# A decoder step on one core: a longer and earlier warm-up of TensorE, the sample rows' transposes placed between the two prompt tiles, and a final norm with its order and owners changed

## What is computed

```python
def rmsnorm(x, g):
    y = x * lax.rsqrt(jnp.mean(x * x, axis=-1, keepdims=True) + EPS)
    return y * g

hp = jnp.concatenate([meta, x_prompt], axis=1)     # 16 + 256 rows
hs = x_sample                                      # 8 rows
mp, Sp, Pp = mixer(rmsnorm(hp, norm_mix), ...)     # w_in, retention, pooling, w_out
hp = hp + mp
hp = hp + moe(rmsnorm(hp, norm_ffn), ...)          # 32 experts, top 4, clamped SwiGLU
...                                                # the same for hs, with the running state
y_prompt = rmsnorm(hp[:, N_META:], norm_final)
y_sample = rmsnorm(hs, norm_final)
```

## Time and profile before

| | |
|---|---|
| median of 3 runs | 1202.28 us (1201.06 to 1202.86) |
| the profiled execution | 1203.43 us, its span in the profile 1201.6 us |
| TensorE (PE) busy | 1154.7 us, 96% of the span |
| VectorE, ScalarE, GpSimd busy | 307.2, 160.0, 62.8 us |
| DMA | 455.09 MB, mean 379 GB/s |
| the chain that ended last | PE 68%, DMA 30%, SP's queue 1% |

### The profile page before, as it was taken

One profiled execution on the slowest core, in us unless ns is written; L12 is line 12 of the kernel. 1 busy time (PEld: TensorE's weight loads), 2 busy tenths in 40 slices (PEclk: granted clock), 3 DMA queues, 4 the chain that ended last, 5 costly groups with the idle time before them and its releaser, 6 DMA issues.

```text
span 1201.6 us, 13661 instructions
## 1 busy us (share of the span) xinstructions
PE 1154.7 (96%) x5403; PEld 572.8 (48%) x5403; DVE 307.2 (26%) x699; ACT 160.0 (13%) x314; POOL 62.8 (5%) x92
## 2 busy tenths in 40 slices
PE   8999999999999999999989998989999989999997
PEld 7888788886434334333434333434333434333332
DVE  4363511232122122221221221213121212121222
ACT  2122111002010111111110101010101100110112
POOL 3252600000000000000000000000000000000000
PEclk9999999999999999999999999999999999999999
DMA  9762788476999999999999999999999999999996
GB/s 321 231 228 90 261 327 319 142 315 264 424 418 427 424 434 428 425 434 425 425 434 426 431 428 434 421 435 426 436 425 433 421 433 429 433 428 429 428 419 241
DMA packets 63728, 455.09 MB, mean 379 GB/s; under 512 B 4321, under 2 KB 35501, under 8 KB 42688
## 3 DMA queue, kind: packets, MB, share of 16 engines
q1 hardware_dynamic: 59168, 439.60, 88.3%
q0 software_dynamic: 4176, 14.34, 3.5%
q10 hardware_dynamic: 344, 0.61, 0.1%
HBM read 448.65 MB, written 6.11 MB: 378 GB/s over the span
## 4 chain that ended last, share of the span: by engine, by line
PE 68%; DMA 30%; SPq 1%; issue 0%; ACT 0%; DVE 0%; DVEq 0%; ACTq 0%
PE psum L1087 24%; DMA ring<-in_w_down 21%; PE psum L1016 19%; PE psum L1098 10%; DMA ring<-in_w_gate_up 8%; PE psum L1174 5%; PE psum L1208 2%; PE psum L1154 1%; SPq L591 1%; PE psum L1164 1%; PE psum L1209 1%; PE psum L1183 1%; DMA ring<-in_x_prompt 0%; PE psum L897 0%; PE psum L1088 0%
## 5 line engine op out<-in xcount | busy, mean ns | idle before, releaser
L1087 PE MATMUL psum<-ring,x_T 128*64 128x512 f32 x1004 | 455.7, 600 | 9.6 <-DMA ring<-in_w_gate_up 8.8
L1088 PE MATMUL psum<-ring,x_T 128*64 128x512 f32 x994 | 450.6, 600 | 0.0
L1087 PEld LDWEIGHTS psum<-ring,x_T 128*64 128x64 f32 x1004 | 131.0, 137 | 275.1 <-issue 252.4
L1098 PE MATMUL psum<-ring,act_T 128*64 128x512 f32 x960 | 216.0, 602 | 25.1 <-DMA ring<-in_w_down 25.1
L1016 PE MATMUL psum<-ring 128*128 128x264 f32 (+1 forms) x768 | 181.7, 392 | 0.6 <-DMA ring<-in_w_in 0.6
L1016 PEld LDWEIGHTS psum<-ring 128*128 128x128 f32 x768 | 143.2, 190 | 30.2 <-ACT qk L1445 2.1
L1098 PEld LDWEIGHTS psum<-ring,act_T 128*64 128x64 f32 x960 | 70.2, 138 | 159.4 <-issue 139.6
L1088 PEld LDWEIGHTS psum<-ring,x_T 128*64 128x64 f32 x994 | 129.6, 137 | 0.0
L1906 DVE TENSOR_TENSOR h_raw<-psum,params 128x512 f32<-128x512 f32 x32 | 22.1, 691 | 295.0 <-PE psum L1154 295.0
L1923 DVE TENSOR_TENSOR z_T<-z_T,psum 128x264 f32<-128x264 f32 x112 | 43.0, 425 | 205.5 <-PE psum L1209 205.5
L1174 PE MATMUL psum<-normed,one_hot 128*128 128x512 f32 x168 | 74.4, 592 | 0.0
(11 more groups left out here) (268 smaller groups left out, 751.3 us busy)
## 6 DMA issues: line engine op xcount, KB each, us to landing
ring<-in_w_gate_up SPq DMA_DIRECT2D x32, 4096.0 KB, 31.7
ring<-in_w_gate_up SPq DMA_DIRECT2D x59, 2048.0 KB, 29.8
ring<-in_w_down SPq DMA_DIRECT2D x56, 2048.0 KB, 33.3
ring<-in_w_in SPq DMA_DIRECT2D x21, 1024.0 KB, 6.6
ring<-in_w_down SPq DMA_DIRECT2D x12, 1024.0 KB, 26.8
spare<-in_w_gate_up SPq DMA_DIRECT2D x5, 1280.0 KB, 36.8
out<-ring POOLq DMA_DIRECT2D x9, 512.0 KB, 9.5
ring<-in_state_ret POOLq DMA_DIRECT2D x8, 512.0 KB, 7.2
```

The source lines that it names most:

```text
L1087: mm(psum[0:CAP, 2 * j + n], x, gate, start=first, stop=final)
L1088: last = mm(psum[CAP:P, 2 * j + n], x, up, start=first, stop=final)
L1098: last = mm(psum[j * CAP:(j + 1) * CAP, 4 + n], hidden[:, j, 4 * h + i], w, start=h == 0 and i == 0, stop=h == 1 and i == 3)
```

## The change

Three places change. `WARM` goes from 6 to 10, and GpSimd clears `k_few` first of all, then `small` and the third tile. The loads of the sample and meta rows move from SP's queue, behind the prompt tiles, to ACT's queue, behind `norm_mix` and ahead of the other three small vectors; SP goes from the prompt tiles to `w_in` at once. Their transposes on TensorE (L954) and the scaling on VectorE (L1693) move between the tiles: after tile 0 and ahead of tile 1. In the final norm the sample piece of the second half comes before that of tile 1; the first square roots and the first reciprocal are those of tiles 0 and 2, and tile 0 is scaled right behind them. Tile 1 is split: ACT scales its first half, VectorE makes its second half in one operation out of PSUM. The sample rows' first half is weighted by VectorE early and scaled by GpSimd, and only their second half is made by VectorE at the end.

```diff
-WARM = 6
+WARM = 10
...
-        Y_HALVES = [(n, t) for n in range(2) for t in (0, 1, 2)]
+        Y_HALVES = [(n, t) for n in range(2) for t in ((0, 1, 2), (0, 2, 1))[n]]
...
-            sp.wait_ge(cleared, 2)
-            sp.dma_start(tok[0:NS, 2, :], x_sample.rearrange("b s d -> (b s) d")).then_inc(x_in[2], 16)
-            sp.dma_start(tok[NS:NS + NM, 2, :], meta).then_inc(x_in[2], 16)
...
+            nc.gpsimd.memset(k_few[:, :], 0.0).then_inc(few_cleared, 1)
             nc.gpsimd.memset(small[:, 0:4], 1.0).then_inc(cleared, 1)
+            nc.gpsimd.memset(tok[:, 2, :], 0.0).then_inc(cleared, 1)
             nc.gpsimd.memset(y_sums, 0.0).then_inc(zeroed, 1)
-            nc.gpsimd.memset(tok[:, 2, :], 0.0).then_inc(cleared, 1)
             nc.gpsimd.memset(place[:, :, :], FAR).then_inc(zeroed, 1)
-            nc.gpsimd.memset(k_few[:, :], 0.0).then_inc(few_cleared, 1)
...
+            pool.wait_ge(y_weighted, 3)
+            pool.wait_ge(y_rstd, 1)
+            nc.gpsimd.tensor_scalar(normed[0:NS, 2, 0:512], normed[0:NS, 2, 0:512], rstd[0:NS, 2:3], None,
+                                    ALU.mult).then_inc(y_s_ready, 1)
...
+            act_e.dma_start(rows[0:8, 0:P], ins["norm_mix"].rearrange("l (a p) -> (l a) p", p=P)).then_inc(norm_in, 16)
+            act_e.wait_ge(cleared, 2)
+            act_e.dma_start(tok[0:NS, 2, :], x_sample.rearrange("b s d -> (b s) d")).then_inc(x_in[2], 16)
+            act_e.dma_start(tok[NS:NS + NM, 2, :], meta).then_inc(x_in[2], 16)
+            for o, name, n in ((8, "ret_gn", 8), (16, "pool_scale", 4), (20, "norm_ffn", 8)):
...
-                    for s in (0, 1) if i == 4 else (2,):
+                    for s in (0, 2) if i == 4 else (1,):
                         A(rms[:, s:s + 1], y_sums[:, 3 + s:4 + s], ACT.Sqrt, bias=y_base[:, s:s + 1],
                           scale=1.0 / D).then_inc(y_rms, 1)
-                act_e.wait_ge(y_weighted, 4)
-                act_e.wait_ge(y_rstd, 1)
-                A(normed[:, 1], normed[:, 1], ACT.Copy, scale=rstd[:, 1:2]).then_inc(y_ready, 1)
-                act_e.wait_ge(y_ready, 1)
+                act_e.wait_ge(y_weighted, 2)
+                act_e.wait_ge(y_rstd, 2)
+                A(normed[:, 1, 0:512], normed[:, 1, 0:512], ACT.Copy, scale=rstd[:, 1:2]).then_inc(y_ready, 1)
+                act_e.wait_ge(y_ready, 2)
...
-                    if t == 2:
-                        continue
-                    V.tensor_tensor(normed[:, t, c], y_tok(t)[:, c], w_final[:, c], ALU.mult).then_inc(y_weighted, 1)
-                    if i == 3:
+                    if i < 4:
+                        rows_n = TILES[t][1]
+                        V.tensor_tensor(normed[0:rows_n, t, c], y_tok(t)[0:rows_n, c], w_final[0:rows_n, c], ALU.mult).then_inc(
+                            y_weighted, 1)
+                    elif i == 4:
                         dve.wait_ge(y_rms, 2)
-                        V.reciprocal(rstd[:, 0:2], rms[:, 0:2]).then_inc(y_rstd, 1)
-                    if i == 4:
-                        dve.wait_ge(y_weighted, 3)
+                        V.reciprocal(rstd[:, 0:3:2], rms[:, 0:3:2]).then_inc(y_rstd, 1)
+                        dve.wait_ge(y_weighted, 4)
                         dve.wait_ge(y_rstd, 1)
                         V.tensor_scalar(normed[:, 0], normed[:, 0], rstd[:, 0:1], None, ALU.mult).then_inc(
                             y_first_ready, 1)
                 dve.wait_ge(y_rms, 3)
-                V.reciprocal(rstd[:, 2:3], rms[:, 2:3]).then_inc(y_rstd, 1)
+                V.reciprocal(rstd[:, 1:2], rms[:, 1:2]).then_inc(y_rstd, 1)
                 dve.wait_ge(y_rstd, 2)
-                for n in range(2):
...
+                V.scalar_tensor_tensor(normed[:, 1, c], y_tok(1)[:, c], rstd[:, 1:2], w_final[:, c], ALU.mult,
+                                       ALU.mult).then_inc(y_ready, 1)
+                V.scalar_tensor_tensor(normed[0:NS, 2, c], y_tok(2)[0:NS, c], rstd[0:NS, 2:3], w_final[0:NS, c], ALU.mult,
+                                       ALU.mult).then_inc(y_s_ready, 1)
```

More of the change, by code:

```diff
@@ L951, in _ @@
                     pe.transpose(psum[:, 2, 0:KD], rows[0:KD, 0:P], ident[0:KD, 0:KD]).then_inc(norm_turned, 1)
-            pe.wait_ge(x_in[2], 32)
-            for k in range(KD):
-                last = pe.transpose(psum[:, 3, k * few:(k + 1) * few], tok[0:few, 2, k * P:(k + 1) * P],
-                                    ident[0:few, 0:few])
-            last.then_inc(few_turned, 1)
+                    pe.wait_ge(x_in[2], 32)
+                    for k in range(KD):
+                        last = pe.transpose(psum[:, 3, k * few:(k + 1) * few], tok[0:few, 2, k * P:(k + 1) * P],
+                                            ident[0:few, 0:few])
+                    last.then_inc(few_turned, 1)
             def turn_roots():
@@ L1403, in _ @@
             act_e.dma_start(consts[:, 0:EARLY], ins["consts"][:, 0:EARLY]).then_inc(ident_in, 16)
-            for o, name, n in ((0, "norm_mix", 8), (8, "ret_gn", 8), (16, "pool_scale", 4), (20, "norm_ffn", 8)):
-                act_e.dma_start(rows[o:o + n, 0:P], ins[name].rearrange("l (a p) -> (l a) p", p=P)).then_inc(
-                    rows_in if o else norm_in, 16)
-            act_e.wait_ge(cleared, 1)
+            act_e.dma_start(rows[0:8, 0:P], ins["norm_mix"].rearrange("l (a p) -> (l a) p", p=P)).then_inc(norm_in, 16)
[3 more added lines that the diff above has]
+            for o, name, n in ((8, "ret_gn", 8), (16, "pool_scale", 4), (20, "norm_ffn", 8)):
+                act_e.dma_start(rows[o:o + n, 0:P], ins[name].rearrange("l (a p) -> (l a) p", p=P)).then_inc(rows_in, 16)
             step(A(small[:, 1:2], small[:, 0:1], ACT.Sqrt))
@@ L1690, in _ @@
                     V.tensor_copy(norm_mix, psum[:, 2, 0:KD]).then_inc(norm_ready, 1)
[L1691 to L1695 removed]
+                    dve.wait_ge(norm_ready, 1)
+                    dve.wait_ge(few_turned, 1)
+                    V.tensor_tensor(x_raw[:, :, NPR:NA], psum[:, 3, 0:KD * few].rearrange("p (k c) -> p k c", k=KD),
+                                    norm_mix.rearrange("p (k c) -> p k c", c=1).broadcast_to([P, KD, few]),
+                                    ALU.mult).then_inc(few_scaled, 1)
             for n in range(2):
```

9 lines of the change are left out of this document (1 added, 8 removed).

## The result

| | before | changed |
|---|---|---|
| median (19 runs of each) | 1202.19 us (1201.06 to 1202.96) | 1203.94 us (1202.08 to 1206.78) |
| ratio, 95% interval | | 1.0017 (1.0011 to 1.0023) |
| the profiled execution, its span | 1203.43, 1201.6 us | 1203.30, 1201.4 us |

By the interval of the ratio the changed kernel is 1.3 to 2.8 us **slower**; by the medians it is 1.75 us. That is within the 0.2% (2.4 us) of the prediction's middle class, but it has the other sign than the forecast of 1201.5, and 1203.94 lies outside the range that ended at 1203.6.

What follows compares the result with a forecast made beforehand. TensorE was taken to bound the kernel to 275 us and the weights' stream from 300 us. Start -0.40 and end -0.35 gave 1202.28 - 0.75 = 1201.5 us (chance 0.55), range 1200.2 to 1203.6.

Steps and rivals of the forecast that it cites:

- the prediction's middle class: Whole kernel: time within 0.2% (2.4 us) of before, neither faster nor slower by more; chance 0.91.
- What bounds the kernel: TensorE to 275 us, weights' stream from 300 us; a microsecond's shift of the start should come out at the end.
- The start: First 9 us: first real matmul at 8.70 instead of 9.10, -0.40 us; ends -0.50 and +0.51.
- X: Start: time when second prompt tile and few rows have both landed; taken as 6.95 us, ends 6.79 and 7.86.
- Rival 2: Start: few rows land late on ACT's queue; with X = 8.0 first matmul at 9.75, +0.65, total 1202.6; chance 0.12.
- The clock: Start: TensorE's clock rises from 1.2 to 2.4 GHz, taken to rise a microsecond sooner with the earlier warm-up.
- The warm-up: Start: begins 1.0 us sooner, at about 1.0, with twenty instructions; tile 0 starts at about 5.2.
- The end: Last 8 us, final norm: stores 0.45, 0.08 and 0.34 us sooner, taken as -0.35; ends -0.45 and -0.08.
- my lower end of 0.08: End: smallest gain expected, -0.08 us, where only the second store counts.
- Rival 1: End: GpSimd gets the port lock before VectorE; end +1.2, with the start's -0.4 +0.8, total 1203.1; chance 0.12.
- my price for 8x512 alone: End: GpSimd's scaling of the sample rows' first half, 1.55 us when running alone.
- The sums: Whole kernel: added-up gains and losses of the cases, from -0.95 to +1.9 us, the latter with rivals 1 and 2 together.

Runs made afterwards that it cites:

- e7: Changed kernel with the few rows (sample and meta) back on SP's queue, ahead of `w_in`: 1202.15 us, ratio 0.9994 to the kernel before.
- e12: Changed kernel plus six idle matmuls, into an unused PSUM bank, ahead of the wait for the few rows: 1204.02 us, ratio 1.0017 to before.
- e2: Kernel before with only the change's final norm, old start: 1201.88 us, ratio 1.0000.
- e1: Changed kernel with the old final norm, so the change's start alone: 1204.04 us, ratio 1.0016 to the kernel before.
- e3: Kernel before with only the few rows' loads moved from SP's to ACT's queue: 1204.38 us, ratio 1.0016.
- e15: Changed kernel unaltered, profiled once more: one execution, 1203.80 us.
- e9: Changed kernel, but SP waits for GpSimd's clearing of `q_only`, so `w_in` is issued behind the few rows: 1202.39 us, ratio 0.9999 to before.
- e8: e7 plus four idle matmuls ahead of the wait for the few rows (output not the reference's): 1202.28 us, ratio 1.0005 to the kernel before.
- e6: Changed kernel plus six idle matmuls over part of tile 0's transposed rows, ahead of the few rows' wait (output wrong): 1203.98 us, ratio 1.0011 to before.
- e5: Kernel before with only the new warm-up (10 matmuls, `k_few` cleared first): 1201.89 us, ratio 1.0000.
- e14: Changed kernel unaltered, profiled once more: one execution, 1203.17 us.

## Why the two profiles don't show the loss

At the turn the changed kernel is 19.24 - 16.72 = 2.5 us late. At the first gather it is 281.49 - 280.46 = 1.03 late. Between the two, before lost 1.5 us in the chain: the same 24 matmuls, first of the kernel before, then of the changed one.

```profile
274.42 4.35 PE psum L1039 x24
```

```profile
276.94 2.68 PE psum L1039 x24
```

The stretch table shows why, before first and then changed:

```profile
275.00:277.00 2.00, 2.00 (x13) 1.90 (x12) 1.79 (x15) 1.11 (x1) 0.00 (x0) 0.56 0.97 418
277.00:279.00 2.00, 2.00 (x14) 1.44 (x11) 0.24 (x1) 1.31 (x2) 0.00 (x0) 0.59 0.97 402
```

```profile
277.00:279.00 2.00, 2.00 (x20) 1.91 (x19) 1.55 (x13) 1.25 (x2) 0.00 (x0) 1.00 0.95 410
```

The profiled execution of before had its own stretch at 1.2 GHz there, 3.4 us long, as e7 and e12 had (turn to gather 263.74 to 263.75 us in these three, 262.24 to 262.25 in the others). TensorE did not stop ahead of it in any of the three; what it ran from 271.6 to 274.4 in the kernel before are narrow matmuls of 1 and 32 columns, and the profiles without the fall have the same ones. So the one profile that I predicted from was of an execution that carried an extra 1.5 us, and the mean of 1.00 over 9 to 275 us ended just ahead of it. Of the 1.03 us that are left, 0.33 come back at the end. The other 0.9 (the spans differ by 0.2 in the changed kernel's favour) is gone from the chain between 340 and 564 us: the same block of the chain, before first and then changed, is 0.17 late.

```profile
564.44 7.09 PE psum L1098 x32
```

```profile
564.61 7.09 PE psum L1098 x32
```

That is inside the weights' stream. From the first gather to the first matmul that adds the last expert pair it is 908.39 to 910.60 us long in the 17 profiles, though their programs are the same there; the changed kernel's own three are 908.52, 909.79 and 909.12. So a single profile can hide or double the shift of the start. The bytes hide it less. Against e2, and read where SP's queue has 340 to 5 MB left to move (ten points), e1 is 1.1 us late on average, e3 2.5, e15 2.6 and e9 0.1 early, close to their shifts at the first gather (1.1, 2.4 and 2.4 late, 0.3 early). By the same measure the changed kernel is still 0.4 to 0.7 us behind the kernel before, and at the first adding matmul it is only 0.10 behind. What makes the last piece vary, from the bytes to that matmul, was not tried.

## Why the prediction was wrong, step by step

**What bounds the kernel** held as far as it could be told: every kernel whose few rows are late is slower, and by the bytes above the shift runs on through the stream. That a shift of the first matmul comes out one for one isn't shown: neither the kernels that start 0.4 us sooner (e7, e9) nor the one that starts 1.0 us later by its fillers (e8) are told from before. And from the first statistics to the first gather single executions differ by 1.5 us, from the clock at 275 us.

**The start** failed, in X. I took 6.95 us for the landing of the few rows with an upper end of 7.86, and measured 8.41 (8.15 to 8.46 in all eight profiles of that order on ACT's queue). The step that failed is the sentence at the end of that part: "SP reaches `w_in` sooner by two issues ... I take nothing for it". I looked only at what that would bring SP's own queue, and not at what the two halves of `w_in`, issued *ahead* of the few rows, do to them on the DMA engines that all queues share: 1.52 us (8.41 against 6.89 in e9). My two ends came from the earlier trace rows of a program in which `w_in` was issued last; neither row could bound the new order. The rest of the step was right: the first matmul comes at X + 1.75 by the working, and at 8.41 + 1.88 in the changed kernel (where the clock fell inside it), 6.89 + 1.80 in e9. In e9 the whole forecast of the start is there, 8.69 for 8.70, but its median (1202.39 beside 1202.18) shows no gain from it.

**Rival 2** was what happened. It was priced at 0.65 for X = 8.0. Its reason, the place behind the identity and `norm_mix`, was not the cause (e9), and its price was too small twice: L1016 at +1.2 instead of +0.65, and the fall of the clock, which none of my cases had.

**The clock** was considered only as a level that rises with the warm-up. That a pause ahead of the second tile could lose it again was not. From the wait alone, 1202.19 + 1.2 - 0.33 = 1203.06, which is below what the interval of the ratio allows (1203.5 to 1205.0); with the fall in every run it would be 1204.4. So the wait alone is too little. How the median divides between the wait and the clock stays open: of the two filled kernels e6 allows the wait alone and e12 does not, and in e8 a first matmul just as late costs nothing that can be told.

**The warm-up** did what it says in that it starts at 1.00 with 20 instructions. Whether the clock has risen by tile 0 varies: e1 and e5 show 1.09 us for its transposes, the changed profile 1.43, e8 1.76. No median shows a gain.

**The end** was right in sum, 0.33 for 0.35. Counted from the first adding matmul, the stores are issued 0.32 sooner, 0.04 later and 0.29 sooner; forecast were 0.45, 0.08 and 0.34 sooner. The first falls short by 0.12: counted from that matmul the reciprocal (L2015) ended 0.06 later than before, as the working had allowed for with the extra weighting, and L2018 began 0.11 us behind it and not 0.05. That the two outer stores moved by a third and the middle one not at all, and the end moved by a third, speaks for the outer stores' gain and against my lower end of 0.08; which of the two outer ones it is, no run parts. In e6 the three stores are issued as early and the end doesn't move: the last packet on ACT's queue, tile 1's store, ends 10.84 us after that matmul, against 9.87 in the changed kernel.

**Rival 1** did not occur in any of the 12 profiles with the new norm: VectorE started first, at 1194.72, and GpSimd at 1194.79. By the Trainium skill ("SBUF — State Buffer", section "SBUF: two separate sides") the one of the two that starts first keeps the port pair for its whole instruction; the page says this of a VectorE instruction in a 2-port mode, or of one with two SBUF inputs beside a GpSimd instruction that reads SBUF. For L2018 the trace agrees: GpSimd's row is 2.12 us long, and 1194.72 + 0.75 = 1195.47 leaves 1.44 of it behind VectorE's end, where my price for 8x512 alone was 1.55. VectorE's next piece, L2024, reads PSUM and one SBUF tile; it ran from 1195.60 to 1196.35 in the middle of GpSimd's row and was not held.

**The range** was narrower than the working under it. The sums reached +1.9 where rivals 1 and 2 meet, which from 1202.28 is 1204.2, but the range ended at 1203.6. The measured 1203.94 lies between the two. It got there by another path, with rival 1 absent and a clock that no sum had, so that the sums would have covered it is luck.

## What to carry to other kernels

- Before a small transfer is moved to an idle queue, write down the *issue times* of everything that shares the DMA engines, before and after. The queue that it leaves moves up too, and the small transfer that was ahead of a big one may now be behind it; a wait of a microsecond on the big one's issue can be free.
- A load that everything waits for should not stand ahead of a step that could have run meanwhile: the same late rows put L1016 off by 0.64 us where the second tile's transposes came first (e3) and by 1.2 where they came behind. Here the medians (1204.38 and 1203.94) don't show that difference, as the clock fell in both profiles.
- Predict from more than one execution if the sums are about a microsecond: one profile of this kernel can carry 1.5 us that its median does not.

## What the runs showed of the hardware that I had not expected

- Two half megabytes issued at 1.68 and 2.14 put the landing of 96 KB, issued on another queue at 1.90 and 2.22, off by 1.5 us (8.41 against 6.89 in e9, where they were issued at 2.95 and 3.38). The first of them landed no sooner for an issue that was 0.9 or 1.3 us earlier (8.9, against 8.55 and 8.45).
- Stops of TensorE (as short as 0.47 and 0.57 us in e3, 1.43 in the changed kernel) were followed by 3.4 us at 1.2 GHz in five of the seven profiles with late few rows and no filler. The same program kept 2.4 GHz in another execution (e14) after a stop longer than e15's.
- The same 3.4 us at 1.2 GHz stood at 275 us in three of the profiles (before, e7, e12), where the rows show no stop of TensorE ahead of it, and cost 1.5 us.
- VectorE was ahead of GpSimd by 0.07 us in all 12 profiles in which one reciprocal released both.
